# A hybrid RG-LRU and sliding-window attention layer: the program laid out anew without barriers, with overlapped stages

## The reference, cut to what matters

```python
h = layer_norm(concat([meta, x], axis=1), ln_emb_g, ln_emb_b)      # 16 + 2048 positions
z = h @ w_in + b_in                                                # 2048 -> 12800 columns
xr, gr, q, k, v, ga, mg = split(z)
# A: causal conv (width 4) -> RG-LRU (block-diagonal gates, scan over positions) -> * silu(gr) -> w_rnn_out
log_a = 8 * sigmoid(x @ w_ra + b_ra) * log_sigmoid(lam)
u = sqrt(1 - exp(2 * log_a)) * sigmoid(x @ w_ri + b_ri) * x ;  h_t = a_t h_{t-1} + u_t
# B: rotary q/k, window of 128 plus the 16 meta tokens, 32 q heads on 4 kv heads, a sink per head in the denominator
o = softmax_with_sink(q k^T / 8) v  -> * silu(ga) -> w_attn_out
out = (sigmoid(mg[:D]) * y_a + sigmoid(mg[D:]) * y_b) @ w_o + b_o
return layer_norm(2**0.25 * h + out, ln_g, ln_b)                   # meta tokens dropped
```

## Time and profile before

| | us |
|---|---|
| median of 3 runs | 3193.03 (3190.34 to 3193.85) |
| profiled execution | 3203.31 |
| its span, slowest core (5) | 3201.6 |
| spans of the eight cores | 3173.7 to 3201.6 |
| PE, DVE, ACT, POOL busy | 2602.6, 1478.3, 1044.2, 347.7 |

### The profile page before, as it was taken

The page is one execution under the profiler, slowest core; times in us unless marked ns, Lnnn a source line. Parts: engine busy times, 40 slices in busy tenths (PEclk is TensorE's granted clock), DMA queues, the critical chain, the costliest instruction groups (busy, mean ns, idle before and its releaser), DMA issues.

```text
span 3201.6 us, 34265 instructions; the slowest of 8 cores (3173.7 to 3201.6 us)
## 1 busy us (share of the span) xinstructions
PE 2602.6 (81%) x11952; PEld 1133.4 (35%) x11952; DVE 1478.3 (46%) x1933; ACT 1044.2 (33%) x1641; POOL 347.7 (11%) x318
## 2 busy tenths in 40 slices
...
GB/s 139 46 64 44 47 47 7 37 53 42 61 49 73 77 78 74 79 145 130 107 149 59 62 40 47 47 7 37 60 53 58 58 76 76 79 73 79 179 97 105
DMA packets 601911, 227.23 MB, mean 71 GB/s; under 512 B 564728, under 2 KB 593784, under 8 KB 594304
## 3 DMA queue, kind: packets, MB, share of 16 engines
...
HBM read 369.73 MB, written 16.78 MB: 121 GB/s over the span
## 4 chain that ended last, share of the span: by engine, by line
PE 69%; DVE 12%; DMA 8%; ACT 5%; issue 4%; another core or an unknown queue 1%; POOL 0%; DVEq 0%; ACTq 0%; SPq 0%; POOLq 0%
PE ps_zb L507 34%; PE ps_sbk L507 11%; PE ps_ob L507 6%; PE ps_db L507 6%; DMA s_wz_all<-w_in 3%; DMA s_rao<-w_o 3%; DVE s_rw L605 2%; PE ps_sbk L528 2%; PE ps_sbk L724 2%; PE ps_ob L604 2%; PE ps_db L604 2%; PE ps_sbk L571 2%; DMA s_rw<-x 1%; PE ps_zb L849 1%; PE ps_zb L468 1%
## 5 line engine op out<-in xcount | busy, mean ns | idle before, releaser
L507 PE MATMUL ps_zb<-s_rh,s_wz_all 128*128 128x512 bf16 (+1 forms) x4256 | 944.7, 378 | 108.1 <-DMA s_wz_all<-w_in 100.4
L507 PEld LDWEIGHTS ps_zb<-s_rh,s_wz_all 128*128 128x128 bf16 x4256 | 401.1, 100 | 621.2 <-issue 192.6
L343 POOL DMA_DIRECT2D s_wz_all<-w_in x192 | 221.5, 1156 | 1291.9 <-PE ps_zb L507 848.2
L507 PE MATMUL ps_sbk<-s_rh,s_wz_all 128*128 128x512 bf16 x1536 | 342.1, 383 | 18.6 <-DVE s_rao L692 18.6
L775 DVE SCALAR_TENSOR_TENSOR s_rw<-s_rw,ps_zb 128x512 f32<-128x512 f32 x64 | 44.0, 687 | 604.9 <-PE ps_zb L507 604.9
L764 ACT ACTIVATE s_rw<-ps_sbk,s_hbin_c 128x512 f32<-128x512 f32 x96 | 66.0, 688 | 690.7 <-PE ps_sbk L507 682.1
L605 DVE RECIPROCAL s_rw<-ps_db 128x512 f32<-128x512 f32 x64 | 214.9, 3357 | 90.7 <-PE ps_db L604 90.7
L507 PE MATMUL ps_zb<-s_rao,s_wz_all 128*128 128x512 bf16 x1024 | 226.2, 379 | 0.0
L507 PEld LDWEIGHTS ps_sbk<-s_rh,s_wz_all 128*128 128x128 bf16 x1536 | 151.6, 99 | 204.1 <-issue 26.7
L849 PE MATMUL ps_zb<-s_rao,s_rw 128*128 128x512 bf16 x384 | 102.0, 433 | 117.6 <-DMA s_rao<-w_o 108.5
L576 ACT ACTIVATE s_ptm<-ps_sbk 16x512 bf16<-16x512 f32 x128 | 68.1, 579 | 278.7 <-PE ps_sbk L571 278.7
...
## 6 DMA issues: line engine op xcount, KB each, us to landing
s_wz_all<-w_in POOLq DMA_DIRECT2D x192, 512.0 KB, 7.7
...
s_wz_all<-w_rnn_out POOLq DMA_DIRECT2D x32, 512.0 KB, 7.4
s_wz_all<-w_attn_out POOLq DMA_DIRECT2D x32, 512.0 KB, 6.5
s_rao<-w_o POOLq DMA_DIRECT2D x8, 2048.0 KB, 55.0
...
```

The lines of the kernel that those rows point to most:

```text
L343: P.dma("pool", wk, lambda e: e.dma_start(out=w[:], in_=w_in_v[:, :, c0:c0 + 128]), writes=[wk])
L507: P.op("pe", (lambda zb, n, kc, cs, w: lambda e: e.matmul(zb[:, 0:n], lhsT=w[:, kc, :], rhs=rhs_fn(kc, cs, n), start=(kc == 0), stop=(kc = ...
```

## The change

Almost all of the program text is new; the mathematics is the same.

- **Dependences.** Tiles are placed by hand at byte addresses of one SBUF tensor `s_all`, and the recording layer finds waits from the bytes and PSUM banks that an instruction touches. There is no barrier but the last. The ring of weight tiles has four slots.
- **Weights** are laid out on the host so that a tile is 128 rows of 8 KB. K is computed once per kv head (2 tiles, not 4). The columns of q and k are ordered so that a pair of tiles holds the two halves of the rotation; `rope` reads both banks with DVE (four bias-and-multiply, two adds), and 8 DMAs (16 for K) of 32 partitions on SP bring the result into place. ACT's copy and the float32 matmul are gone.
- **Head.** Gain and bias are applied by DVE in 2048-wide operations, to bfloat16; the transposes are bfloat16, 8 to a bank, emptied by one ACT instruction. V, K and the first Q tile are computed between blocks.
- **Attention.** The exponential of minus the logarithm replaces the reciprocal, both on ACT. Two meta scores become one matmul, two masks become one of 1024 columns. The sigmoid of the attention gate is exp(-ln(1+exp(-z))) on ACT (`ga_tile`) and no longer a tanh. Group kh's items run beside group kh+1's q tiles and gate tiles; the last group's beside four "late" gate tiles and the first two conv input tiles.
- **RG-LRU.** Scan and scaling of the round before stand between the two convolutions of a round; one root for both halves; the scan is in place.
- **Merge.** `side` puts between its tiles: the residual ALPHA * norm(x) + b_o of this pass, written to a DRAM tensor `r_s`; in pass 0 the norm and transposes of pass 1's x, written to `ht_s`; and half of w_o.
- **Output.** The other half of w_o is loaded when `hT` has been read for the last time; the block's residual is loaded; sums for the norm are taken chunk by chunk on ACT.
- ACT's tables are loaded by explicit instructions (`table`), of which there are 47.

```diff
-            P.barrier()
-            P.dma("pool", "wv", lambda e: e.dma_start(out=wv[:], in_=w_in_v[:, :, OFF_V:OFF_V + 256]), writes=["wv"])
-            preload(load_kdup(0))
-            preload(load_kdup(1))
...
-                        P.op("dve", lambda e: e.reciprocal(out=rden, in_=DB[:, :]), reads=["DB0", "DB1"], writes=[pfx + "rden"])
...
+            t1, t2, t3, t4 = [r[:, 0:n] for r in rt]
+            stt(t1, zA[:, 0:n], bA, c, ALU.add, ALU.mult)
+            stt(t4, zA[:, 0:n], bA, s, ALU.add, ALU.mult)
+            stt(t2, zB[:, 0:n], bB, s, ALU.add, ALU.mult)
+            stt(t3, zB[:, 0:n], bB, c, ALU.add, ALU.mult)
+            tt(d[:, 0, 0:n], t1, t2, ALU.subtract)
+            tt(d[:, 1, 0:n], t3, t4, ALU.add)
...
+            act(lt[:], db, AF.Ln)
+            act(lt[:], lt[:], AF.Exp, scale=-1.0)
...
+            w = wtile(w_in_d[TGA + j])
+            for cs, n in chunks:
+                zb = next_z()
+                z_mm(zb, w, cs, n)
+                pump()
+                i = gctr[0] % 2
+                gctr[0] += 1
+                z, s = gz[i][:], gs[i][:]
+                ts(z, zb, bin_c[:, TGA + j:TGA + j + 1], -80.0, ALU.add, ALU.max)
+                act(s, z, AF.Exp, scale=-1.0)
+                act(s, s, AF.Ln, bias=ONE_T)
+                act(s, s, AF.Exp, scale=-1.0)
+                dst = og[:, j, cs - OFF:cs - OFF + n]
+                if late:
+                    tt(s, z, s, ALU.mult)
+                    tt(dst, s, dst, ALU.mult)
+                else:
+                    tt(dst, z, s, ALU.mult)
...
+        rate[0] = 17.0 / 16.0
+        for kh in range(3):
+            att_q.extend(att_items(kh))
+            budget[0] = 0.0
+            qk = q_pair(kh + 1, 0)
+            qk(0)
+            qk(1)
+            ga_tile(4 * kh + 4, False)
+            ga_tile(4 * kh + 5, False)
+            qk = q_pair(kh + 1, 1)
+            qk(0)
+            qk(1)
+            ga_tile(4 * kh + 6, False)
+            ga_tile(4 * kh + 7, False)
+            while att_q:
+                att_q.pop(0)()
+        att_q.extend(att_items(3))
+        rate[0] = 17.0 / 11.0
+        for j in range(4):
+            ga_tile(j, True)
...
+        for nb in range(1, 8):
+            decay(nb - 1)
+            xr_tile(2 * nb)
+            roots()
+            conv(2 * nb)
+            scan(2 * nb - 2)
+            scan(2 * nb - 1)
+            xr_tile(2 * nb + 1)
+            conv(2 * nb + 1)
+            load_wg(nb)
+            gr_tile(2 * nb - 2)
+            gr_tile(2 * nb - 1)
+            gates(nb)
+        decay(7)
...
+        def merge_c(c):
+            if c > 0:
+                mg_tile(c, tA, TMG + c)
+                mg_tile(c, tB, TMG + 16 + c)
+            side(2 * c)
+            y_tile(c, w_att_d, og, tB, False)
+            side(2 * c + 1)
+            y_tile(c, w_rnn_d, AT, tA, True)
...
+            stt(y, zb, 0.5, y, ALU.mult, ALU.add)
+            s = sums[tb % 3]
+            act(jk[0], y, AF.Identity, accum=s[:, cg, 0:1])
+            act(jk[1], y, AF.Square, accum=s[:, cg, 1:2])
```

1582 lines of the change are left out of this document (841 added, 741 removed).

## The result

The changed kernel takes 2640 us (2639.95 and 2640.26) where the kernel before takes 3188.62 to 3193.85: a ratio of **0.827, 95% interval 0.825 to 0.829**. In its other two runs one die had a lower granted clock (2674.43 and 2925.96 us); such runs are left out here and in the experiments. The prediction said 2525 with 2400 to 2700: the direction is right, the gain is 550 us where 665 were forecast, and the time is 115 us (4.6%) above the number named, 20 us above the forecast's own range of 2450 to 2620.

A forecast was written before the change was run, and what follows sets the result against it. PE's matmuls, 2280 us, were the floor, with uncovered head and tail and partly exposed ACT-DVE chains. Pass 0 1306, pass 1 1212 and tail 15 gave 2533, adjusted to 2527, said as 2525; own range 2450 to 2620, eight-in-ten range 2400 to 2700.

The forecast's parts named there:

- head, to the first scores: Start of pass 0: norms, set-up and first K rotation 99 us, then remaining projections; first attention loop begins at 134.
- loops, pass 0 / 1: Three attention loops a pass: 84 us each, between 75 with ACT-DVE chains covered and 87 exposed; 252 in all.
- late tiles and gap: After the loops: last kv group under four late gate tiles 55 us, then conv input tiles and first gates 30.
- RG-LRU, 7 rounds: RG-LRU stage: DVE's order and two tanh buffers set 35 us a round, 36.5 in pass 0; 255 and 245.
- merge: Merge stage: PE-bound, 64 tiles plus two late gate tiles 456 us; pass 1's transposes make it 466 in pass 0.
- output: Output stage: 110.5 us of PE plus 3 us of waiting for w_o, 113.5 in each pass.
- start of pass 1: K, Q and V at pass 1's start, plus 5 us for rope tables queued behind the last store: 60 us.
- tail: End of the kernel: a norm of 9 us and a store of 5.4, together 15 us.
- rival B: RG-LRU rounds and gate stretches: PE falls to 1.2 GHz after small gaps, 90 us more, 2620; chance 0.25.
- rival A: Whole kernel: ACT and DVE chains hidden, PE the bound, rounds 32.6 and 31.1 us, total 2392; chance 0.17.
- Rival C: Whole die: clock held down when all engines are busy, up to 478 us, total 2850 to 3000; chance 0.05.
- Rival D: Weight tiles through one POOL queue: at 9.6 us a tile, 700 us more, slower than before; chance 0.02.

The follow-up runs named there:

- Run 11: Changed kernel plus four tanh buffers, later column clearing, undrained loop ends, earlier gate-chunk eviction, early first-norm constants and sink rows, early pass-1 tables: 2485.7 to 2486.9 us.
- experiment 1: Changed kernel with the attention gate's last product issued on DVE one chunk later: 2641.5 to 2642.0 us, ratio 0.8245 to the kernel before.
- experiment 3: Changed kernel with the gate chunk moved out of its bank before the attention step is issued: 2575.6 to 2578.6 us, ratio 0.8078 to the kernel before.
- experiment 5: Changed kernel with four buffers instead of two for the tanh of the RG-LRU's gates: 2591.7 to 2594.7 us, ratio 0.8093 to the kernel before.
- experiment 6: Changed kernel with a2's first column cleared behind the convolution, not ahead of it, in pass 0: 2618.5 to 2631.6 us, ratio 0.8190 to the kernel before.

## Why the prediction was right where it was, and where it was wrong

| step | predicted us | measured us |
|---|---|---|
| head, to the first scores | 134 | 162 |
| loops, pass 0 / 1 | 252 / 252 | 253 / 253 |
| late tiles and gap | 85 / 85 | 86 / 90 |
| RG-LRU, 7 rounds | 255 / 245 | 289 / 250 |
| merge | 466 / 456 | 472 / 456 |
| output | 113.5 / 113.5 | 112 / 112 |
| start of pass 1 | 60 | 78 |
| tail | 15 | 21.5 |

The sum missed 113 us, and four terms make 86 of them: the head 28, the RG-LRU of pass 0 34, the start of pass 1 18, the tail 6.5. Eight more are the 0.3% that the prediction took off because the median before lay below its profiled run: here the two agree. The rest is a few us a stage. All of these lie on the same side. The range of 2400 to 2700 held because it was wide; the forecast's own range did not.

Two of the signs named as the forecast's came out otherwise: the clock in attention was not 1.00, and there is a wait over 10 us after the head, 14.0 at the start of pass 1.

- **Head: terms mis-sized, and one left out.** The last norm ends at 113.9 us where 99 was forecast. Nine of these 15 us are the constants: the meta block was to end near 22 and ends at 31.5, because its second operation waits for them:

```profile
29.21 2.34 DVE L412 SCALAR_TENSOR_TENSOR s_all<-s_all 16x2048 bf16<-16x2048 f32 x1 [3.82 <-DMA s_all<-be_bc]
```

  Most of the others pass between norm 7 and norm 8, where DVE stands 4.5 and 2.0 us for PE in K's first rotation. From the last norm to the first scores it is then 48 us where 35 were forecast. In the forecast only K's second chunk and three Q pairs, 27.6 us, were left for after the norms; in fact 206 matmuls of 512 columns, 44.5 us, stood behind 94.9 us. The moves of q and k, which the prediction did not price at all, add a wait of 4.4 us: SP issues 40 in 27.6 us, 0.69 each. The sink rows stand behind them in SP's queue; ACT waits for them, DVE 11.2 us for ACT, and PE 3.3 us for DVE. Run 11 shows that the constants were not the only thing in the way: with them early the head was 3 us shorter, because x came late. Three views of that stretch: PE's groups by form from 94.9 to 163.8 (count, busy, mean ns, idle before), SP's queue, and PE's first scores.

```profile
L424 PE MATMUL ps<-s_all 128*128 128x512 bf16 x206 | 49.4, 399 | 12.1 <-DVE s_all L412 11.9
```

```profile
95.23 27.60 SPq L533 DMA_DIRECT2D s_all<-s_all  x40
122.89 2.79 SPq L433 DMA_DIRECT2D s_all<-sink_rows  x2
```

```profile
162.06 2.34 PE L424 MATMUL ps<-s_all 64*128 64x512 bf16 x6 [4.38 <-DMA s_all<-s_all]
```

- **Loops: size right, price of the parts wrong.** The chain per pair was put at 12.5 us against 9.4 of PE; measured 10.6 against 9.5. The culprit named was the product's wait; experiment 1 shows that it costs nothing, experiment 3 that it is L408's place in DVE's queue. Of a loop's 84 us some 76 to 77 are PE (75 forecast), about 4 are waits, about 3 the clock after them. That they come to the 84 named is luck: the 9 us a loop that the forecast booked as exposed chain were 4 of waits, 3 of a clock that it had put at nothing, and 1 to 2 of PE's own work.
- **The clock: rival B was not a rival but a part.** "Attention at clock 1.00" is wrong: 0.96. In the six stretches of loops, late tiles and rounds the clock took some 61 us from the matmuls, against B's 90, and the measured 2640 lies nearer to B's 2620 than to 2525. What the prediction held against B, that the new gaps are 3 us where the old ones were 9 to 10, did not help: 2 to 3 us were enough. In the loops the forecast had taken the same us as exposed chain. Experiments 3 and 5 show that both go together: where the gaps close, the clock returns to 0.99 or 1.00.
- **RG-LRU: pass 1 right with its mechanism** (the two tanh buffers, experiment 5: 35.7 to 32.1 us, near rival A's 31.1). In pass 0 the clearing of the column, which must wait for the root, was not seen, 3.3 us a round (experiment 6); after it 38.0 are left against the forecast's 36.5. With both changes it is 34.4, so the forecast of 36.5 is near in size but not a floor.
- **Merge: pass 1 exact**, and clock 1.00 in all of it. In pass 0 the transposes of pass 1's norms were put at 10 us and the merge takes 16 more than in pass 1. The transposes themselves are eight groups of 16, 1.06 us each, 8.4 us in all; before four of them PE waits for DVE's norm, 6.5 us, which the forecast had put at nothing:

```profile
1048.30 1.06 PE L489 MATMUL ps<-s_all 128*128 128x128 bf16 x16
```

```profile
PE ps L489 <- DVE s_all L412: 6.5, 4, 2.1
```

- **Output: right.** One wait for w_o of 1.4 us where 3 were forecast.
- **Start of pass 1: seen, and priced too low.** The forecast gave 5 us to the rope tables queued behind the last store. PE begins pass 1 at 1375.64 and stops after three chunks of K, 48 matmuls, because DVE's rotation cannot empty the banks before the cosine table has landed, at 1398. PE stands 14.0 us for it, and 3.1 later. With the tables early, in run 11, the two waits are 1.8 and 4.6 us.

```profile
1375.64 10.74 PE L424 MATMUL ps<-s_all 128*128 128x512 bf16 x48
1400.37 29.96 PE L424 MATMUL ps<-s_all 128*128 128x512 bf16 x126 [13.99 <-DVE s_all L412]
```

```profile
1398.23 0.75 DVE L412 SCALAR_TENSOR_TENSOR s_all<-ps,s_all 128x512 f32<-128x512 f32 x1 [7.97 <-DMA s_all<-cos_t]
```

- **Rival C** is refuted for this result: from 800 to 980 and from 2060 to 2500 us all eight cores had PE at 617 to 620 of 620 us and clock 1.00, and the profiles of this kernel hold no level but 1.2 and 2.4 GHz. The rule of the Trainium skill ("TensorE: Matmul & The Clock Gate", Part 1), a die at 13/16 of the clock once three of its cores run dense matmuls, is not seen in these windows. The level itself does exist: two cores of a die had 0.81 in experiment 6, in attention loops and not in a merge, and the other two had not. What sets it off is not shown. **Rival D** is refuted too: tiles land in 6.0 us.
- **Tail: the store mis-sized.** The norm and the store were put at 9 and 5.4 us. DVE ends the norm at 2625.9 us, 9 after PE's last matmul; from there to the end of the span it is 12.5.

Where the 550 us came from, by single undoing: the barriers 128, exp(-ln) 92, layout and ring 41 to 47, hand-loaded tables about 0. These are some 265 us, more or less if they overlap. The other half (rotary from PSUM, each K rotated once, the norms under the merge, w_o loaded early) was not undone one by one and is only argued from the order.
